# Prompt attention: TensorE's step reordered to turns, scores, values with its waits at the head, and scores written key tile by key tile

## What is computed

```python
s_c = jnp.einsum('bqhgd,bchd->bhgqc', q, kc).astype(F32) * scale
p_c = masked_softmax(s_c, c_end[None, :] <= q_pos[:, None])
o_c = jnp.einsum('bhgqc,bchd->bqhgd', p_c, vc.astype(F32))
...
s_s = jnp.einsum('bqhgd,bqhkd->bhgqk', q_rot, k_s).astype(F32) * scale
o_s = jnp.einsum('bhgqk,bqhkd->bqhgd', masked_softmax(s_s, m_s), v_s.astype(F32))
...
s_w = jnp.einsum('bqhgd,bkhd->bhgqk', q_rot, kv_w[:, :, 0]).astype(F32) * scale
o_w = jnp.einsum('bhgqk,bkhd->bqhgd', masked_softmax(s_w, m_w), kv_w[:, :, 1].astype(F32))
o = gates[..., 0:1] * o_c + gates[..., 1:2] * o_s + gates[..., 2:3] * o_w
```

## Time and profile before

| | |
|---|---|
| median of 3 runs | 2426.31 us (2425.86 to 2426.57) |
| the profiled execution's own time | 2428.94 us |
| its span | 2427.0 us |
| TensorE busy | 2331.1 us, 96% |
| VectorE busy | 870.3 us, 36% |
| ScalarE busy | 596.9 us, 25% |
| GpSimd busy | 341.1 us, 14% |
| mean granted TensorE clock | 0.98 |

### The profile page before, as it was taken

One profiled execution on the slowest core, in us unless ns is written; L12 is line 12 of the kernel. 1 busy time (PEld: TensorE's weight loads), 2 busy tenths in 40 slices (PEclk: granted clock), 3 DMA queues, 4 the chain that ended last, 5 costly groups with the idle time before them and its releaser, 6 DMA issues.

```text
span 2427.0 us, 27761 instructions
## 1 busy us (share of the span) xinstructions
PE 2331.1 (96%) x9646; PEld 1347.1 (56%) x9646; DVE 870.3 (36%) x1714; ACT 596.9 (25%) x1288; POOL 341.1 (14%) x762
## 2 busy tenths in 40 slices
PE   8998999799999999999999999899999999999976
PEld 6455656576566666666665556454454554454522
DVE  0217888632356663000102558311111111111139
ACT  2126666544243332000000220011111111111111
POOL 0003444201000000000000000122322322322300
PEclk9998999999999999999999999999999999999978
DMA  6210000336221103111103121199999999998856
GB/s 208 97 70 28 1 1 1 142 136 243 73 70 35 31 26 106 39 39 39 35 18 102 61 81 75 60 340 344 349 349 338 349 343 345 349 342 337 328 223 265
DMA packets 127081, 389.55 MB, mean 161 GB/s; under 512 B 20628, under 2 KB 77932, under 8 KB 98304
## 3 DMA queue, kind: packets, MB, share of 16 engines
q1 hardware_dynamic: 105360, 304.02, 34.2%
q0 software_dynamic: 21632, 84.31, 9.4%
HBM read 362.02 MB, written 50.04 MB: 170 GB/s over the span
## 4 chain that ended last, share of the span: by engine, by line
PE 89%; DVE 6%; issue 2%; DMA 1%; ACT 1%; SPq 1%; ACTq 0%; DVEq 0%
PE PS L1071 25%; PE PS L1293 19%; PE PS L1304 9%; PE PS L665 8%; PE PS L778 5%; PE PS L1206 4%; PE PS L811 3%; PE PS L848 2%; PE PS L1190 2%; PE PS L948 2%; PE PS L1245 1%; PE PS L713 1%; PE PS L1029 1%; PE PS L1342 1%; DMA arena<-in_win 1%
## 5 line engine op out<-in xcount | busy, mean ns | idle before, releaser
L1071 PE MATMUL PS<-arena 128*128 128x344 f32 x2112 | 612.9, 452 | 3.7 <-ACT arena L1624 3.1
L1071 PEld LDWEIGHTS PS<-arena 128*128 128x128 f32 x2112 | 400.9, 190 | 214.3 <-issue 3.8
L1293 PE MATMUL PS<-arena 128*128 128x512 f32 x1056 | 464.3, 592 | 0.0
L1353 ACT ACTIVATE arena<-PS 128x512 f32<-128x512 f32 (+12 forms) x561 | 267.4, 502 | 686.4 <-PE PS L665 435.3
L665 PEld LDWEIGHTS PS<-arena 128*128 128x128 f32 (+3 forms) x1960 | 238.6, 160 | 211.0 <-issue 133.8
L665 PE MATMUL PS<-arena 128*128 128x128 f32 (+3 forms) x1960 | 292.9, 281 | 37.2 <-DVE arena L1857 8.1
L1293 PEld LDWEIGHTS PS<-arena 128*128 128x128 f32 x1056 | 196.1, 191 | 221.1 <-issue 221.0
L1304 PE MATMUL PS<-arena 128*128 128x512 f32 x528 | 242.9, 592 | 0.0
L2213 DVE TENSOR_TENSOR arena<-PS,arena 128x256 f32<-128x256 f32 x66 | 28.0, 425 | 437.9 <-ACT arena L1675 437.9
L1304 PEld LDWEIGHTS PS<-arena 128*128 128x128 f32 x528 | 95.5, 191 | 94.7 <-issue 94.7
L2278 POOL TENSOR_SCALAR arena<-arena 128x384 f32<-128x384 f32 (+3 forms) x192 | 103.7, 564 | 141.2 <-DVE arena L1834 95.8
(11 more groups left out here) (308 smaller groups left out, 2059.5 us busy)
## 6 DMA issues: line engine op xcount, KB each, us to landing
arena<-in_w_exp_gate SPq DMA_DIRECT2D x66, 1024.0 KB, 7.0
arena<-in_w_exp_up SPq DMA_DIRECT2D x66, 1024.0 KB, 9.2
arena<-in_w_exp_down SPq DMA_DIRECT2D x66, 1024.0 KB, 8.6
arena<-expert_rows SPq DMA_DIRECT2D x8, 3072.0 KB, 11.9
arena<-in_w_in SPq DMA_DIRECT2D x34, 512.0 KB, 3.7
arena<-in_x_prompt SPq DMA_DIRECT2D x16, 512.0 KB, 4.3
arena<-in_w_in SPq DMA_DIRECT2D x16, 256.0 KB, 7.5
arena<-in_win SPq DMA_DIRECT2D x8, 512.0 KB
```

The lines of the kernel that those rows point to most:

```text
L1071: ins = mm(PS[:, bank + c, 0:CH], w[:, k, :], rhs[:, k, c * CH:(c + 1) * CH], start=k == 0, stop=k == kts - 1)
L1293: ins = mm(PS[:, 2 + s, :].rearrange("p (h n) -> p h n", h=2), xgT[:, s, k, :], wex[:, :, s, k, :], start=k == 0, stop=k == KT - 1)
L1353: return fn(out, in_, ACT.Copy)
```

## The change

In `scores`, a unit of selected or window keys is no longer one matmul per group, but one matmul of 128 columns per key tile and group, the groups alternating. The waits inside `turn_probs` and `values` are taken out. TensorE's step k now begins with the waits for the scaling of unit k-6 and for both copies of unit k-7, then does the turns of unit k-6, the scores of unit k, and the values of unit k-7. Before, the step was scores, turns, values. VectorE's step k now begins with the copy of unit k-6, and the maxima of unit k and the coefficients come behind it. Before, the copy stood behind them.

```diff
-                    for g in range(2):
-                        ins = mm(PS[:, b + g, 0:n], qrT[GP[g], u["j"], q], kvT[GP[g], col, c0:c0 + n], start=True, stop=True)
+                    for c in range(0, n, P):
+                        for g in range(2):
+                            ins = mm(PS[:, b + g, c:c + P], qrT[GP[g], u["j"], q], kvT[GP[g], col, c0 + c:c0 + c + P], start=True, stop=True)
                 E.do(ins, qk_done)
...
-                pe.wait_ge(scale_done, k + 1)
-                if k:
-                    pe.wait_ge(pt_ev[0], k)
...
-                        if g and N_PT1[k] > 1:
-                            pe.wait_ge(pt_ev[1], N_PT1[k] - 1)
...
-                pe.wait_ge(pt_ev[0], k + 1)
...
-                    pe.wait_ge(pt_ev[1], N_PT1[k])
...
             for k in range(NU + LAG + 1):
+                if k == LAG:
+                    pe.wait_ge(tokT_ready, 3 * NT)
+                if 0 <= k - LAG < NU:
+                    pe.wait_ge(scale_done, k - LAG + 1)
+                if 0 <= k - LAG - 1:
+                    pe.wait_ge(pt_ev[0], k - LAG)
+                    if N_PT1[k - LAG - 1]:
+                        pe.wait_ge(pt_ev[1], N_PT1[k - LAG - 1])
+                if 0 <= k - LAG < NU:
+                    turn_probs(k - LAG)
...
-                if k == LAG:
-                    pe.wait_ge(tokT_ready, 3 * NT)
-                if 0 <= k - LAG < NU:
-                    turn_probs(k - LAG)
                 if 0 <= k - LAG - 1:
                     values(k - LAG - 1)
...
             for k in range(NU + LAG + 3):
-                if k < NU:
-                    maxima(k)
-                if k == 1:
-                    rope_queries(NT - 1)
-                if 1 <= k <= NU and (UNITS[k - 1]["kind"] == "c" or UNITS[k - 1]["last"]):
-                    coefs(k - 1)
                 if 0 <= k - LAG < NU and UNITS[k - LAG]["kind"] != "c":
...
                     E.do(V.tensor_copy(PTs[:, (k - LAG) % 2, 1, 0:w], PS[:, 5, 0:w]), pt_ev[1])
+                if k < NU:
+                    maxima(k)
+                if k == 1:
+                    rope_queries(NT - 1)
+                if 1 <= k <= NU and (UNITS[k - 1]["kind"] == "c" or UNITS[k - 1]["last"]):
+                    coefs(k - 1)
```

## The result

The changed kernel is slower: 2437.67 us, median of 7 runs (2432.66 to 2443.34), against 2426.31 for the kernel before, now the median of 7 runs too (2423.67 to 2431.3). The ratio is 1.0044, with a 95% interval of 1.003 to 1.0058. That is 11.4 us, inside the stated range of 2435 to 2456; the forecast of 2444 had the loss at 18.

What follows compares the result with a forecast made beforehand. TensorE was taken as the bound, with almost no slack. Loops in i=7 to 4 (16.2 us), scores in i=3 to 0 (0.8) and start and end (1) made 18.0, added to the 2426.31 median: 2444, range 2435 to 2456.

Steps and rivals of the forecast that it cites:

- loops of two steps: Attention blocks i=7 to 4: scaling and ScalarE's copy end in turns, then scores two units on; 16.2 us in all, 0.82.
- The wait before the first unit's turns: Block i=6: the scaling path needs 3.80 us where TensorE has 3.05 to fill, so it stands 0.75.
- The scores' split: Scores by key tile: 4 tiles take 1.09 us against 1.06, some 0.01 a tile, 2.6 over 264 tiles.
- loads do not hide: Rival for the split scores: weight loads show fully, 0.10 us a tile, 36 in all, so 2462; chance 0.06.
- The group of i=6: Four units of one head pair in block i=6: 11.01 us against 9.90 before, +1.1 a group.
- the hand-overs: Passing from one engine to the next in the loop paths: estimated 0.1 us each, half or double giving -2 to +3.
- i=4: Attention block of units with 3, 2, 3, 2 tiles: 9.99 us a group against 8.54, +1.45, the largest share.
- compressed units: I carry the 12.1 us over, with nothing gained: Waits for VectorE's copy behind compressed units stay at 12.1 us; the range takes -4 to +4 for them.
- four groups each: Blocks i=7 to 4: each of four groups pays its loop, 2.4, 4.4, 3.6 and 5.8 us, together 16.2.
- the +1 for start and end: Attention's start, where first scaled turns hold back scores, and end, where turns wait for both copies: +1 us.
- The next stage: After attention: its loads start later by as much as attention ends later; TensorE still stands 5.70 us, nothing given back.
- faster: Rival: the waits for VectorE's copy vanish, -12.1 us and +2.6 for the scores, so 2417; chance 0.06.

Runs made afterwards that it cites:

- ScalarE's edit: Changed kernel with ScalarE's copy of unit k-6 ahead of the exponentials, now of unit k-1: attention stage 274.2 us, median 2434.2 us, ratio 1.0035.
- both edits together: Changed kernel with ScalarE's copy one place ahead and, in i=7 to 4, VectorE's coefficients of a finished group ahead of the next maxima: stage 269.3 us, ratio 1.0015.
- TensorE's order alone: Kernel before with TensorE's step as turns, scores, values, waits at its head, scores unsplit, VectorE's copy unmoved: attention stage 427.5 us, 2584.0 us (1 run).

## Why the prediction was right, and where its size was off

The mechanism was right and is shown: with turns ahead of scores, the paths over scaling and over ScalarE's copy become loops of two steps. The wait before the first unit's turns was put at 0.75 and is 0.66, before the third unit's at 0.36 and is 0.22; ScalarE's edit takes away the second, both edits together the first as well.

- **The scores' split.** 1.09 for 4 tiles was forecast and measured, where the rival "loads do not hide" had 1.47. It is out.
- **The group of i=6**: 11.01 forecast, 10.78 measured. 0.12 of the difference is a row read wrongly: in the earlier trace rows ACT's copy at 260.55 was taken for the end of the exponentials, but it waited for the turns that begin at 259.97. Here, with the turns long done, copy follows exponentials after 1.13 (262.99 to 264.12), where I had 1.25 (259.30 to 260.55 in the kernel before). The rest is mostly the hand-overs, put at 0.1: the turns follow the scaling after 0.02 (259.50 to 259.52) and the copy after 0.09 (264.61 to 264.70).
- **i=4** was the largest error among the blocks, 5.8 us forecast. The next two rows are scores of that block in the kernel before, one group apart:

```profile
334.58 0.92 PE L811 MATMUL PS<-arena 64*128 64x384 f32 x4
...
343.35 0.92 PE L811 MATMUL PS<-arena 64*128 64x384 f32 x4
```

  8.77 us, not the 8.54 that I added up from blocks: PE already waited a little there. In the changed kernel:

```profile
347.83 0.94 PE L812 MATMUL PS<-arena 64*128 64x128 f32 x12
...
357.58 0.60 PE L812 MATMUL PS<-arena 64*128 64x128 f32 x6
```

  9.75 us against a forecast of 9.99. So +0.98 a group, not +1.45: of the 0.47, 0.23 are the kernel before and 0.24 the loop.
- **The step that was mis-sized most is "compressed units: I carry the 12.1 us over, with nothing gained"**, and "four groups each". The first group behind a compressed unit waits in both kernels, and the waits replace each other instead of adding up. In i=6 the kernel before loses 0.75 and 0.77 us there (the turns at 231.50 and at 234.49, above, which take 1.33 and 1.79 to the next block, where 0.58 and 1.02 are their own pace). The changed kernel loses 1.32 in one piece:

```profile
233.21 0.88 PE L842 MATMUL PS<-arena 128*64 128x128 f32 x12
...
235.34 0.88 PE L665 MATMUL PS<-arena 128*128 128x128 f32 x6 [1.26 <-POOL arena L2278]
```

  (2.13 for a block of 0.81). So the first group waits 0.2 us less than before, where I had it cost 1.1 more. Three groups of a block pay the loop, not four. From one block's compressed scores to the next's (starts of the L806 rows), i=6 took 46.80 us for 44.12, i=5 43.47 for 40.85, i=4 42.67 for 39.57: +2.7, +2.6 and +3.1, where 4.4, 3.6 and 5.8 were forecast. i=7 came out at +2.8, with 2.4 forecast, and i=3 to 0 about even instead of at +0.8; the +1 for start and end is not to be seen as a term of its own. That is the whole difference between 18 and 11.
- **The next stage** gives nothing back, as forecast: PE stands 6.40 us for its loads, where it was 5.70, so they cost slightly more.
- **The rival "faster"** saw something true: its 12.1 us could be had, but not with this order. Moving the copy only as far as between maxima and coefficients took 6.8 us off the stage.

Not tried: a longer distance between scores and turns (a larger LAG), and VectorE's copy between maxima and coefficients together with TensorE's new order. No run shows what they would do.

## What to carry to other kernels

Where an engine works at its own pace with no waits, an exchange of two pieces in its step is not free: count for each thing that the moved piece waits for how much work lay ahead of it before and lies ahead of it now, and close the loop through every engine's own order. When shortening one path, work out the next one beneath it first: here two edits gave 1.1 and 2.7 us apart and 7.2 together in the blocks i=6 to 4. And in an engine's step, the result that is awaited soonest goes first among those that are ready: the copy ahead of the coefficients took 6.8 us off the stage.

A gain or loss of one or two us is read from a stretch at one clock level, not from a stage that opens at the lower level for a length that varies. And a label that names one engine for a wait on several is checked against that engine's own rows.

## What the runs showed of the hardware

A change of PE's tile shape seems to have a price that I had not looked for. In the kernel before, the turns (128*128) are now and then followed by values of a compressed unit (also 128*128) instead of those of another unit (128*64). Eight turns and what follows:

```profile
247.55 1.09 PE L665 MATMUL PS<-arena 128*128 128x128 f32 x8
...
248.48 1.02 PE L841 MATMUL PS<-arena 128*128 128x512 f32 x2
```

They take 0.93 to the next block, where eight turns ahead of 128*64 values take 1.02 (257.73 to 258.75 in the earlier trace rows). Two turns take 0.28 (439.20 to 439.48) against 0.36 (440.86 to 441.22). So 0.08 to 0.09 us go with the change of shape (argued from these rows, not tested by a run of its own; the rows cannot tell the change itself from the start of a 64-column block). If each of the three changes in a unit costs as much, an estimate from these rows, that makes 25 to 28 us over 104 units, in either order of the step. The Trainium skill (TensorEngine Tiling (Array Packing), "Key Properties") says that changing the tiling mode drains TensorE; the rows fit that, and give the size.

PE's granted clock was lower where PE stood often. With TensorE's order alone it was busy 136.5 of 200 us at a granted clock of 0.86; in the kernel before, busy 192.2 of the same 200 us, it had 1.00.
